# The delta heads of a hybrid trunk: GpSimd's wide operations in thirds, and five pieces of work in other places

## The reference

```python
qkv = jax.nn.silu(centred_conv(qkv, conv_w))            # 4 taps along the tokens
q = l2norm(q) * DN_DK ** -0.5;  k = l2norm(k)
decay = jnp.exp(jnp.where(incl, gc[..., :, None] - gc[..., None, :], NEG))
a_mat = where(strict, bc[..., None] * kk * decay, 0) + eye
u, w = triangular_solve(a_mat, [vc * bc, kc * bc * exp(gc)])
qk = einsum(qc, kc) * decay;  qg = qc * exp(gc);  kd = kc * exp(gc[-1:] - gc)
def step(S, ...):                                       # over the chunks of one direction
    v_new = u_c - w_c @ S
    o = qg_c @ S + qk_c @ v_new
    S = S * gl_c + kd_c.T @ v_new
o = rmsnorm(o_f + o_b) * silu(z)                        # forward and backward, then w_out
```

## Time and profile before

| | us |
|---|---|
| median of the three runs | 3733.95 |
| the profiled execution, its own time | 3739.49 |
| its span, from the first instruction to the last | 3737.7 |
| TensorE busy in the span | 3344.0 (89%) |
| VectorE busy | 2001.9 (54%) |
| GpSimd busy | 1144.6 (31%) |
| ScalarE busy | 1044.5 (28%) |

### The profile page before, as it was taken

One profiled execution on the slowest core, in us unless ns is written; L12 is line 12 of the kernel. 1 busy time (PEld: TensorE's weight loads), 2 busy tenths in 40 slices (PEclk: granted clock), 3 DMA queues, 4 the chain that ended last, 5 costly groups with the idle time before them and its releaser, 6 DMA issues. The chain is left out here.

```text
span 3737.7 us, 51893 instructions
## 1 busy us (share of the span) xinstructions
PE 3344.0 (89%) x20310; PEld 3185.9 (85%) x20310; DVE 2001.9 (54%) x2743; ACT 1044.5 (28%) x1619; POOL 1144.6 (31%) x797
## 2 busy tenths in 40 slices
PE   4985699899999999779999989989898999999996
PEld 2982489799999999678888878878787999999995
DVE  8757653653444335856776776776746222232217
ACT  3226440311111111243534534434423111111110
POOL 2213101321212112245654654654533121121211
PEclk7997799999999999889999999999999999999998
DMA  4520101121211121131231231231320111111111
GB/s 166 185 101 8 59 1 43 71 79 63 90 63 68 63 85 63 68 84 39 67 67 40 66 80 26 67 80 26 99 86 29 46 41 46 41 46 40 41 46 68
DMA packets 103577, 237.92 MB, mean 64 GB/s; under 512 B 8108, under 2 KB 61132, under 8 KB 100428
## 3 DMA queue, kind: packets, MB, share of 16 engines
q1 hardware_dynamic: 103372, 234.82, 20.0%
HBM read 217.54 MB, written 17.26 MB: 63 GB/s over the span
## 5 line engine op out<-in xcount | busy, mean ns | idle before, releaser
L55 PE MATMUL psum<-h_high,panel_high 128*128 128x384 f32 x3624 | 1249.7, 345 | 99.8 <-DVE h_low L495 76.7
L56 PE MATMUL psum<-h_low,panel_high 128*128 128x384 f32 x3624 | 1226.5, 338 | 0.0
L57 PE MATMUL psum<-h_high,panel_low 128*128 128x384 f32 x3624 | 1225.8, 338 | 0.0
L187 POOL TENSOR_TENSOR panel_low<-panel_raw,panel_high 128x1024 fp32r<-128x1024 f32 x196 | 486.3, 2481 | 1715.2 <-ACT panel_high L182 1670.4
L55 PEld LDWEIGHTS psum<-h_high,panel_high 128*128 128x128 f32 x3624 | 691.7, 191 | 145.6 <-issue 94.1
L56 PEld LDWEIGHTS psum<-h_low,panel_high 128*128 128x128 f32 x3624 | 693.0, 191 | 0.0
L57 PEld LDWEIGHTS psum<-h_high,panel_low 128*128 128x128 f32 x3624 | 691.7, 191 | 0.0
L847 DVE TENSOR_TENSOR ffn_product<-ffn_silu_gate,psum 128x1152 f32<-128x1152 f32 x44 | 59.6, 1354 | 709.9 <-PE psum L57 708.5
L182 ACT ACTIVATE panel_high<-panel_raw 128x1024 fp32r<-128x1024 f32 x195 | 205.1, 1052 | 628.5 <-PE psum L57 561.1
L55 PE MATMUL psum<-ffn_mid_high,panel_high 128*128 128x384 f32 x1056 | 355.3, 336 | 12.2 <-DVE x L650 7.5
L57 PE MATMUL psum<-ffn_mid_high,panel_low 128*128 128x384 f32 x1056 | 354.3, 335 | 0.0
(11 more groups left out here) (336 smaller groups left out, 4812.1 us busy)
## 6 DMA issues: line engine op xcount, KB each, us to landing
panel_raw<-in_stream SPq DMA_DIRECT2D x197, 512.0 KB, 3.3
ffn_mod_panels<-in_wmod SPq DMA_DIRECT2D x24, 1024.0 KB, 7.6
dn_rep<-blocks_spill SPq DMA_DIRECT2D x16, 1152.0 KB, 7.8
in_mod_panels<-in_wmod SPq DMA_DIRECT2D x16, 1024.0 KB, 5.5
dn_qg<-rows_spill SPq DMA_DIRECT2D x16, 576.0 KB, 15.9
first_mod_panels<-in_wmod SPq DMA_DIRECT2D x8, 1024.0 KB, 14.0
x<-in_x SPq DMA_DIRECT2D x3, 1536.0 KB, 14.3
x<-in_x SPq DMA_DIRECT2D x1, 4608.0 KB, 15.5
```

Of the source, the lines that this page charges most:

```text
L55: pe.matmul(out, wh, xh, start=first, stop=False)
L56: pe.matmul(out, wh, xl, start=False, stop=False)
L57: return pe.matmul(out, wl, xh, start=False, stop=last)
L187: pool.tensor_tensor(self.wl[buf][:], self.raw[buf][:], self.wh[buf][:].bitcast(F32), ALU.subtract).then_inc(self.split_low.sem, 1)
```

## The change

The change makes each of the wide GpSimd operations of the heads out of smaller instructions, moves work of other engines to other places, and frees one wait:

- GpSimd: `exponents`, the diagonal blocks, `qg`, `kd` and `gated` become three instructions over 384 columns, `split` two over 512. The semaphore is raised by the last piece.
- TensorE: the turn of k (`nine(1, dn.kn, None, True)`) moves from behind `tile(3, 1)` to before `tile(3, 0)`; `spread(dn.osq)` moves behind `tile(3, 0)`; q's `sums` move behind `tile(3, 1)`. ScalarE takes the turned k (`take(dn.k_tok, 1)`) earlier, and VectorE's count for q's roots changes with it.
- VectorE: the expansion of d = 1 moves from slot 4 to slot 1, and the steps m = 1 to 3 of v's convolution move one slot back.
- The first tap of k's convolution moves from VectorE (at t = 2) to ScalarE (at t = 1).
- `fin` goes to banks 0 and 1; TensorE's wait for its copies moves from step 0 to the next head's panel, where bank 0 is written again (in `ahead` at m == 24).
- SyncE issues the first broadcast (into qn's buffer) as soon as qk's product is done; the second still waits for u.

```diff
@@ sync, in body(h)
                     sp.wait_ge(qg_ready, 2 * h + 2)
+                    sp.wait_ge(grp_full, full_count(h, FULL_QK, True))
+                    rows(h + 1, 0, dn.rows[0]).then_inc(rows_full, 16)
                     sp.wait_ge(u_full, 2 * h + 2)
-                    for d in range(2):
-                        rows(h + 1, d, dn.rows[d]).then_inc(rows_full, 16)
+                    rows(h + 1, 1, dn.rows[1]).then_inc(rows_full, 16)
@@ gpsimd
             def split(h, j):
-                s.pool_split(pool, 4 * h + (p0 + j), (p0 + j) % 2)
+                p, buf = 4 * h + (p0 + j), (p0 + j) % 2
+                pool.wait_ge(s.split_high.sem, p + 1)
+                for half in (slice(0, 512), slice(512, 1024)):
+                    i = pool.tensor_tensor(s.wl[buf][:, half], s.raw[buf][:, half], s.wh[buf][:, half].bitcast(F32),
+                                           ALU.subtract)
+                i.then_inc(s.split_low.sem, 1)
+
+            def thirds(op):
+
+                for n in range(0, NT, 3):
+                    i = op(slice(n, n + 3))
+                return i
...
-                    pool.tensor_tensor(r, r, mask(dn.low[:, d, :], NT), ALU.add).then_inc(dec_ready, 1)
+                    thirds(lambda n: pool.tensor_tensor(r[:, n], r[:, n], mask(dn.low[:, d, :], 3), ALU.add)
+                           ).then_inc(dec_ready, 1)
...
-                    mul(dn.qg[d][:], dn.qn[:], dn.qg[d][:]).then_inc(qg_ready, 1)
+                    qg, qn = by_block(dn.qg[d]), by_block(dn.qn)
+                    thirds(lambda n: mul(qg[:, n], qn[:, n], qg[:, n])).then_inc(qg_ready, 1)
@@ tensor
                     if m == (24 if k_reads == 1 else 40):
                         pe.wait_ge(k_read, k_reads)
+                    if m == 24 and k_reads > 1:
+                        pe.wait_ge(fin_ready, 2 * k_reads - 2)
...
                 read(READ_KK)
+                nine(1, dn.kn, None, True).then_inc(grp_full, 1)
+                read(READ_V)
+                tile(3, 0)
+                read(READ_KTR)
                 if not first:
                     pe.wait_ge(post_step, 2 * h - 1)
                     spread(dn.osq).then_inc(post_full, 1)
-                read(READ_V)
-                tile(3, 0)
+                tile(3, 1)
                 pe.wait_ge(sq_ready["q"], h + 1)
                 sums(7, dn.kd[0]).then_inc(l2_full, 1)
-                tile(3, 1)
+                tile(3, 2)
                 if not first:
                     pe.wait_ge(post_step, 2 * h)
-                nine(1, dn.kn, None, True).then_inc(grp_full, 1)
-                tile(3, 2)
                 pe.wait_ge(recip, 2 * h + 2)
-                read(READ_KTR)
                 spread(dn.kd[0]).then_inc(l2_full, 1)
...
-                    mm = pe.matmul(psum[:, 3 + d, 0:P], blk(dn.kd[d], 0), blk(dn.ub[d], 0), start=True, stop=True)
+                    mm = pe.matmul(psum[:, d, 0:P], blk(dn.kd[d], 0), blk(dn.ub[d], 0), start=True, stop=True)
...
-                    if t == 0:
-                        pe.wait_ge(fin_ready, 2 * h + 2)
@@ scalar
+                        act.wait_ge(k_read, h + 2)
+                        act.activation(dn.kn[:], dn.raw["k"][:], ACT.Copy, scale=at_head(dn.conv, 1, h + 1, 2)
+                                       ).then_inc(conv_step["k"], 1)
@@ vector
-            V_STEPS = {0: (0,), 1: (1,), 2: (2,), 3: (3,), 5: (4,), 6: (5,), 7: (6,)}
+            EXPAND = 1
+            V_STEPS = {0: (0,), 2: (1,), 3: (2,), 4: (3,), 5: (4,), 6: (5,), 7: (6,)}
...
-                        if d == 0 and c == TURN - 2:
+                        if d == 0 and c == EXPAND:
...
-                k_steps = {2: (0,), 3: (1, 2), 4: (3, 4), 5: (5, 6)}
+                k_steps = {3: (1, 2), 4: (3, 4), 5: (5, 6)}
```

More of the change, by code:

```diff
@@ L1930, in exponents @@
                     pool.wait_ge(rows_full, 32 * h + 32)
[L1931 to L1933 removed]
+                    thirds(lambda n: pool.tensor_tensor(
+                        r[:, n], r[:, n], dn.gc_next[:, d, n].rearrange("p (n o) -> p n o", o=1
+                                                                        ).to_broadcast([P, 3, P]), ALU.subtract)
+                           ).then_inc(dec_step, 1)
                     pool.wait_ge(dec_step, 3 * h + (d + 2))
[L1935 removed]
+                    thirds(lambda n: pool.tensor_tensor(r[:, n], r[:, n], mask(dn.low[:, d, :], 3), ALU.add)
+                           ).then_inc(dec_ready, 1)
             split(0, 1)
@@ L1955, in kd @@
                         pool.wait_ge(kd_ready, 2 * h + 1)
-                    mul(by_block(dn.kd[d]), by_block(dn.k_tok), const(EK_, d)).then_inc(kd_ready, 1)
+                    to, k_tok, decay = by_block(dn.kd[d]), by_block(dn.k_tok), const(EK_, d)
+                    thirds(lambda n: mul(to[:, n], k_tok[:, n], decay[:, n])).then_inc(kd_ready, 1)
                 def decayed():
@@ L1982, in gated @@
                     pool.wait_ge(post_step, 2 * h)
-                    mul(dn.osum[:], dn.osum[:], dn.silu_z[:]).then_inc(y_done, 1)
+                    o, z = by_block(dn.osum), by_block(dn.silu_z)
+                    thirds(lambda n: mul(o[:, n], o[:, n], z[:, n])).then_inc(y_done, 1)
                 for d in range(2):
                     pool.wait_ge(decay_act, 4 * h + (d + 1))
-                    mul(by_block(dn.ub[d]), by_block(dn.pt[d]), mask(dn.diag[:], NT)).then_inc(dec_ready, 1)
+                    to, pt = by_block(dn.ub[d]), by_block(dn.pt[d])
+                    thirds(lambda n: mul(to[:, n], pt[:, n], mask(dn.diag[:], 3))).then_inc(dec_ready, 1)
                 split(h, 3)
@@ L2266, in body @@
                     pe.wait_ge(s.split_low.sem, p0 + 4 * DN_H + 1)
+                    pe.wait_ge(fin_ready, 2 * h + 2)
                     for c in range(LAST):
@@ L2373, in body @@
                 take(dn.raw["v"], 0)
+                full(FULL_KTR)
+                take(dn.k_tok, 1)
                 if not first:
@@ L2381, in body @@
                 root(dn.kd[0], 7, D).then_inc(grp_read, 1)
-                full(FULL_KTR)
-                take(dn.k_tok, 1)
                 used(h, 3)
@@ L2429, in body @@
                 for d in range(2):
-                    act.activation(dn.fin[d], psum[:, 3 + d, 0:P], ACT.Copy).then_inc(fin_ready, 1)
+                    act.activation(dn.fin[d], psum[:, d, 0:P], ACT.Copy).then_inc(fin_ready, 1)
                 for t in range(4):
```

7 lines of the change are left out of this document (1 added, 6 removed).

## The result

| | before | after |
|---|---|---|
| median of four runs, us | 3732.74 (3726.13 to 3744.80) | 3675.22 (3670.37 to 3679.49) |
| the profiled execution, us | 3739.49 | 3670.37 |
| start of the first head in it | 1613.37 | 1610.09 |
| first head | 163.24 | 152.80 |
| second to seventh head, mean | 138.00 | 129.73 |

The profiled executions stand 69.1 us apart, since that of before lies above its median and that of after is the fastest of four. Of the 69.1, 65.8 lie in the heads and behind them: 10.4 in the first head, 49.6 in the six that follow, 5.8 from the eighth on.

What follows compares the result with a forecast made beforehand. TensorE was taken as the bound, busy 125.11 of a head's 136.84 us. Gains of 3.6 us in seven heads and 1.4 in the last made 26.6, so 3733.95 would become 3707; range 3693 to 3716, chance 0.48.

Steps and rivals of the forecast that it cites:

- The scan: Smaller GpSimd pieces and earlier first broadcast shorten collisions with k's convolution pairs: gain 2.2 us a head, lower bound -1.2.
- 5.06 together; that is the upper bound of the gain: Scan: two late pairs of k's convolution steps lose 3.37 and 1.69 us over a free pair's 1.54.
- The front: Work up to the first expansion: gain 0 a head, bounds -0.7 and +1.2 us; VectorE's chain stays the bound.
- collide with pieces of split and gate that together are longer than the whole ones: Front: VectorE's first substitution steps meet GpSimd pieces, three times 1.05 against 2.5 us; used in counting the front at 0.
- The clock: Longer TensorE pause before the first turn lowers the clock at the slots: -1.0 us a head, bounds +1.28 and -4.9.
- the fifth head's 2.44 us: Clock price at the slots in the kernel before's fifth head, expected in every head after the change.
- Slots and fin: Slots of d = 0: earlier second expansion gains 1.8 us; before the scan: no wait for fin's copies, 0.6.
- The first head: Counted among the seven heads that prepare a next one, each given a gain of 3.6 us.
- The last head: No convolution of k there, so only fin, slots and clock count: 0.6 + 1.8 - 1.0 = 1.4 us.
- the larger one: Rival: exponents end before the second pair, clock costs no more; 6.7 us a head, 3684; chance 0.16 (below 3693).

Runs made afterwards that it cites:

- whole_scan: The changed kernel with GpSimd's exponents and the split behind them in the scan whole again, all else kept; 3686.02 us, ratio 0.9883.
- whole_front: The changed kernel with GpSimd's diagonal blocks, gate and the front's two splits whole again, the scan's pieces kept; 3687.38 us, ratio 0.9886.
- old_order: The changed kernel with TensorE's and ScalarE's front in the order of before (k's turn, osq's spread, q's sums), pieces kept; 3673.88 us, ratio 0.9843.
- late_sub: The changed kernel, with GpSimd's substitution waiting until VectorE's is through and the second expansion in slot 3; 3658.80 us, ratio 0.9806.
- warm18: The changed kernel with 18 extra matmuls in TensorE's pause before the first turn, their result overwritten; 3675.96 us, ratio 0.9839.
- thirds_only: The kernel before with GpSimd's smaller pieces in front and scan and nothing else of the change; 3685.02 us, ratio 0.9882.
- sep_rows: The changed kernel with a separate semaphore for each of the two broadcasts, so the first exponents need not wait for the second; 3675.99 us, ratio 0.9851.
- moves_only: The changed kernel with all GpSimd operations whole: only the moved work, fin's banks and the early broadcast; 3703.95 us, ratio 0.9927.

## Why the prediction was wrong, point by point

*The scan, forecast 2.2, measured 4.59.* The mechanism was right: the price of a collision is one GpSimd instruction. The step that failed is "5.06 together; that is the upper bound of the gain", as what there was to gain. The gain stayed below 5.06, but it came out of more, and less was left over. The 5.06 was read in the second head; over heads 2 to 7 the pairs of before stand 5.71 us over their free 1.54 each. After, 2.23 of that is left, where the working left some 2.9: 3.48 gained instead of 2.2. Two terms were put at nothing. One is the way from a vn to the next pair: a pair follows a vn by 2.8 us where TensorE still has fill ahead of its update, and by 2.03 where it was waiting for that vn; over three pairs 7.26 before, 6.68 after: 0.58. The other is the clock: the last step at half speed in two heads of six is 0.52. Together 4.58. whole_scan, where long waits and the low clock return together in four heads, agrees that the second is a price of the waits; that every long wait has it is not so, as the last section tells.

*The front, forecast 0, measured 1.63, outside the bounds.* The prediction names a front that ends over a microsecond earlier as a sign that it is wrong. Two numbers came out as worked: the first blocks start at 14.05 us of the head (14.0 forecast), q's reciprocal at 30.16 (30.2). The step that failed is the sentence that the first steps of the substitution "collide with pieces of split and gate that together are longer than the whole ones". It counts the length of what is collided with, and not how many steps get in between. Four instead of two are done when the gate ends; whole_front, with whole operations, is back at two, and the expansion ends at 49.21. That what q's reciprocal gains reaches the end of the front was wrong as well: old_order moves the reciprocal by 0.8 us and the end by 0.1; late_sub, which takes GpSimd's substitution out of VectorE's way, moves the end by 3.2. How the 1.63 divides between the steps that get in and the later turns with GpSimd's substitution, which itself begins 0.9 us earlier in the second head after, is not shown: a fifth step by the end of the gate, in old_order, was worth the 0.1 alone.

The Trainium skill (SBUF — State Buffer, "Who interferes with whom") says that a VectorE instruction with two SBUF inputs contends with a GpSimd instruction that reads SBUF, for ports that it calls an exclusive lock. The rows agree: the same step of the substitution takes 2.66 us beside a whole operation and 0.99 beside a third.

*The clock, forecast -1.0, measured -0.33.* The mechanism was right: every head after the first is slow now, and matmuls in the pause (warm18) take the loss away. The rule of the Trainium skill that was weighed there (TensorE: Matmul & The Clock Gate, "HAM oscillation — how this bites in real kernels"), that work behind every such pause starts at the lower clock, agrees with the rows: behind pauses of 4.5 to 4.7 us each of heads 2 to 7 has its low stretch. The size was not right: a slow head was taken at the fifth head's 2.44 us and costs 1.38, since the fifth head's stretch lay on the slots and the new ones begin in the pause itself. Against thirds_only, with the same end of the front and the shorter pause, the step costs 0.93 (5.24 against 6.17), close to the term; but the kernel before paid 1.05 of the 1.38 already. Where the stretch begins is worth nearly as much again, as sep_rows shows: 0.8 us a head.

*Slots and fin, 1.8 and 0.6, measured 1.51 and 0.86.* Right but for size. About 0.5 of the slots is the pieces' (19.43 in thirds_only), as much the moves' (19.47 in moves_only), and the rest needs both.

*The first head* was given 3.6 like the six behind it and gained 10.4, 2.2 more than they did. There TensorE's first turn came 1.9 us behind the first expansion, at 74.96 us of the head, and comes right behind it now, at 72.99. That is the order's, not the pieces': in old_order it comes at 75.03 again.

*The last head* has no convolution of k; it was given 1.4 and gained 5.0 by its seventh vn, 3.6 of it ahead of the scan as in the others, and 1.4 in the scan's first steps, where the clock of before stood at 0.50 from 104.6 to 108.0 us of that head.

Of the rivals, the larger one came nearest in time (3684), but for another reason: its condition that the exponents are over before the second pair did not hold (they end at 1883.0, the pair starts at 1882.47), and the clock cost 0.33 more a head than before.

## What to carry to other kernels

When a VectorE step with two SBUF inputs stands beside a run of GpSimd instructions, count how many steps get in, one behind each instruction, and not only the length of the run; making the instructions shorter helps even where it makes the run longer. Read a collision in all repetitions of a loop before calling it a bound: one head was not the mean. And where TensorE waits, look at the granted clock of the stretch behind the wait before pricing the wait by its length: the second price can be as large as a collision, and it can take back a gain made elsewhere.

## What the runs showed of the hardware

In whole_scan the four heads with a TensorE wait of 2.0 to 2.3 us in the scan had 3.4 us at a granted clock of 0.50 behind it, the two with 1.2 and 1.5 had none; in the kernel before a wait of 3.08 in the fifth head had none either, so the length of a wait alone does not tell. Small instructions of the two engines take turns: VectorE's substitution steps on 99 to 45 columns take 0.39 to 0.52 us beside GpSimd's (after) and 0.21 to 0.26 alone (late_sub); that cost 3.2 us of each front, more than whole operations cost a head there (1.7, whole_front). And 18 idle matmuls in TensorE's pause kept the clock at 1.00 without making the run shorter.
